# Experts' rows summed in open PSUM banks instead of scattered through HBM, with the overflow pass moved to the middle and two norms taken from one power step

## The chip, the core and the metric

The kernel runs on one NeuronCore of a Trainium2 chip. Its time is the device time of one execution in microseconds (us). The core has a matrix engine (TensorE, in the rows PE, with its weight loads as PEld), a vector engine (VectorE, DVE), a scalar engine (ScalarE, ACT), GpSimd (POOL), and a queue engine (SyncE, SP) that only starts transfers here. Each runs its own instruction list in order, and semaphores tie them together. Transfers between HBM and SBUF share 16 DMA engines. Matmuls write into PSUM, which has 8 banks of 128 x 512 f32.

## What is computed

A block of a language model on 256 tokens of 1024 channels: a first layer with two sequence mixers, then a mixture of experts, a norm, a second layer with a pooling mixer, and a wide convolutional FFN. Cut to what matters here:

```
x = x + gate1 * mix                       # end of the sequence mixers
h2 = modulate(rmsnorm(x, norm2_w), shift2, scale2)
# experts: top group of 4, then top 2 of its 8 experts for each token
hid = silu(xs @ w1[e]) * (xs @ w3[e])     # w1, w3: 32 x 1024 x 512, f32
ys = (hid @ w2[e]) * gate                 # w2: 32 x 512 x 1024, f32
ffn = segment_sum(ys, token)              # two rows for every token
x = rmsnorm(x + gate2 * ffn, final_norm_w)
h = rms_norm(x, norm_mix_g_2)             # a norm of a norm
x = x + pool_mixer(h)
x = x + conv_ffn(rms_norm(x, norm_ffn_g_2))   # 1024 -> 2 x 2816 -> 1024
```

The weights of the 32 experts are 6 MB each, 192 MB in all, and each is read once. Each token has 2 rows, so an expert has 16 rows on average.

## The kernel before

The program is one list per engine, written by hand; what stands first on an engine runs first. **The order of the stages** is: the mixers (to about 285 us of the span), the routing (to about 304), the experts (to about 805), the norms and the pooling mixer (to about 851), the FFN (to the end).

**Routing.** The normed rows are stored by ACT to HBM as `rows_scratch`, twice, one copy for each of a token's two choices (L1578). DVE and PE work out for every expert a block of 64 slots: `places(blk)` (PE L748, DVE L1202) turns rank and expert into `idx`, the token for each slot. Block 0 is needed before the first expert. Blocks 1 to 3 serve only an overflow, experts with more than 64 rows, and are made by an "aside" after the fourth expert (i == 3), together with `fcol`, the turned taps of the FFN.

**Experts.** For expert i POOL gathers 64 rows with an indirect DMA (L1832), four experts ahead. PE turns them (`turn_x`, L793), DVE scales and shifts them (L1258, L1261). PE does `up(i)` (L804 for w1, L807 for w3, side by side in the two halves of the array; every f32 matmul is two instructions), ACT the silu (L1607), DVE the product (L1269), PE `turn_h` (L817), DVE a copy (L1275), PE `down(i)` (L827, L828), DVE the product with gate2 (L1283), and POOL scatters the 128 half rows into `pair_scratch` in HBM (L1838). PE's order in one turn of the loop is up(i+1), turn_h(i), turn_x(i+2), down(i), [aside at i == 3]. PSUM banks are taken in turn, all eight.

**Weights.** SP loads w1, w3 and w2 in halves of 1 MB (L1990, L1992) into 7 slots of 2 MB, in the order w2(i), w1(i+2), w3(i+2). A load waits until PE has used the half that lies in its slot, and SP stands still in order behind it: first halves of w1 behind `down_half(i)`, of w3 behind `up_half(i+2)`.

**Behind the experts** each engine reads the overflow flag and jumps over the overflow pass (96 more blocks), which these inputs don't need. POOL waits for all scatters and sets `joined` (L1824). ACT then loads the pairs back (L1618, 4 x 512 KB). DVE adds them to X with their gates (L1308, L1313), multiplies by the final norm's weight (L1317), and ACT takes the sums of squares (L1416, L1625). The norm of a norm takes two power steps one after the other: POOL (L1697, L1699) takes a power, DVE refines it in four steps (`newton`, L949 to L955). ACT scales the rows for the mixer (L1629). PE, after idle matmuls (`turn_over`, L424), does the mixer's band products (L860, L861, L865) and the pooled products (L877). Then come the third norm, its transposes (L887), and the FFN. Its matmuls (L891 to L893) are fp32r on a high and a low part: ACT casts the high part (L1637), DVE subtracts for the low one (L1373; the first is POOL's, L1873). SP loads the mixer's constants (`late`, L2028, and `pool_w`, L2031) and the FFN's weights (L2052) only after the pairs are in.

## Time and profile before

| | us |
|---|---|
| three runs | 1046.86, 1050.27, 1054.45 (median 1050.27) |
| the profiled execution's own time | 1045.93 |
| its span | 1044.1 |
| mean granted TensorE clock | 0.967 |

| engine | busy, us | share of the span |
|---|---|---|
| PE | 910.6 | 87% |
| DVE | 365.8 | 35% |
| ACT | 199.0 | 19% |
| POOL | 176.1 | 17% |

In 40 slices of 26 us each (digits are tenths, DMA is the busy share of the 16 DMA engines):

```profile
PE   7997999999968979998788887887887489999998
DVE  1244412232342242222121121221221557888843
PEclk9998999999989979999999999999999689999999
DMA  9968326367596999999999999999994884555511
```

From slice 13 to 30 the DMA engines are full: these are the experts' weights. There PE is busy for some 80%, and a share of 80% says that it waits, not for whom. Slice 31 is the stretch after the last expert, where PE is nearly idle. From slice 33 on PE is full and DMA half used: the FFN. A gain in one of these stages is read from the wait that ends last in that stage.

### The profile page before, as it was taken

To read this page: it belongs to the slowest core of one execution; us is meant where nothing else is said; L and a number is where in the kernel's file an instruction comes from. 1 tells how busy PE (TensorE), PEld (TensorE's weight loads), DVE (VectorE), ACT (ScalarE), POOL (GpSimd) and SP (SyncE) were. 2 spreads that over 40 slices of the span, in tenths; PEclk is the share of its full clock that TensorE was granted. 3 is DMA by queue.
4 is the path that set the end of the run, shared out by engine and by line. 5 is a ranking of instruction groups with operands and counts; after the bars stand their busy time and mean duration, and the time that the engine had idled before them with its cause. 6 is when DMAs were issued, how large, how long until landed. Compare 5 with 4: busy or idle time off the path is not lost.

```text
span 1044.1 us, 11655 instructions
## 1 busy us (share of the span) xinstructions
PE 910.6 (87%) x4763; PEld 557.1 (53%) x4763; DVE 365.8 (35%) x631; ACT 199.0 (19%) x296; POOL 176.1 (17%) x188
## 2 busy tenths in 40 slices
PE   7997999999968979998788887887887489999998
PEld 5785656664533443443233232332332379999987
DVE  1244412232342242222121121221221557888843
ACT  1125211211120000000000000000000335555532
POOL 0000645021020120110111101101101222232300
PEclk9998999999989979999999999999999689999999
DMA  9968326367596999999999999999994884555511
GB/s 344 254 167 229 125 81 212 112 242 282 203 385 238 416 405 401 406 401 399 404 410 409 421 404 398 410 414 408 409 419 171 277 278 140 183 163 186 211 47 41
DMA packets 91349, 300.26 MB, mean 288 GB/s; under 512 B 13451, under 2 KB 37507, under 8 KB 66583
## 3 DMA queue, kind: packets, MB, share of 16 engines
q1 hardware_dynamic: 82295, 286.63, 73.4%
q10 hardware_dynamic: 3872, 8.58, 2.2%
q0 software_dynamic: 5120, 4.22, 1.4%
q8 instruction: 40, 0.66, 0.3%
q14 instruction: 22, 0.18, 0.0%
HBM read 300.43 MB, written 11.53 MB: 299 GB/s over the span
## 4 chain that ended last, share of the span: by engine, by line
PE 59%; DMA 33%; DVE 2%; ACT 2%; issue 2%; POOL 1%; ACTq 0%; SPq 0%; POOLq 0%; DVEq 0%
DMA ring<-in_w_dram 19%; DMA arena<-in_w_dram 11%; PE ps L804 7%; PE ps L440 7%; PE ps L891 6%; PE ps L892 6%; PE ps L893 6%; PE ps L807 4%; PE ps L429 4%; PE ps L514 4%; PE ps L827 3%; PE ps L691 3%; PE ps L424 2%; PE ps L450 2%; PE ps L466 1%
## 5 line engine op out<-in xcount | busy, mean ns | idle before, releaser
L807 PE MATMUL ps<-ring,proj 128*64 128x512 f32 x288 | 129.8, 596 | 26.0 <-DMA ring<-in_w_dram 26.0
L1269 DVE TENSOR_TENSOR proj<-RQ,ps 64x512 f32<-64x512 f32 x32 | 22.1, 690 | 298.8 <-ACT RQ L1607 268.0
L804 PE MATMUL ps<-ring,proj 128*64 128x512 f32 x272 | 124.3, 597 | 0.2 <-DMA ring<-in_w_dram 0.2
L807 PE MATMUL ps<-arena,proj 128*64 128x512 f32 x224 | 105.1, 617 | 20.1 <-DMA arena<-in_w_dram 20.1
L804 PE MATMUL ps<-arena,proj 128*64 128x512 f32 x240 | 113.6, 616 | 3.6 <-issue 3.6
L1607 ACT ACTIVATE RQ<-ps 64x512 f32<-64x512 f32 x32 | 18.9, 591 | 472.2 <-PE ps L807 472.2
L1838 POOL DMA_INDIRECT pair_scratch<-MX,idx x32 | 32.4, 1012 | 424.4 <-DVE MX L1283 424.4
L891 PE MATMUL ps<-h_h,w_h 128*128 128x256 f32 x352 | 101.0, 287 | 1.7 <-DVE h_l L1365 1.7
L892 PE MATMUL ps<-h_l,w_h 128*128 128x256 f32 x352 | 100.8, 286 | 0.0
L893 PE MATMUL ps<-h_h,w_l 128*128 128x256 f32 x352 | 100.8, 286 | 0.0
L1373 DVE TENSOR_TENSOR w_l<-ring,w_h 128x2048 fp32r<-128x2048 f32 x32 | 73.3, 2292 | 50.6 <-ACT w_h L1637 50.6
L807 PEld LDWEIGHTS ps<-ring,proj 128*64 128x64 f32 x288 | 37.4, 137 | 83.5 <-DMA ring<-in_w_dram 46.1
L827 PE MATMUL ps<-ring,proj 128*64 128x512 f32 x152 | 68.7, 595 | 13.9 <-issue 13.9
L1637 ACT CAST w_h<-ring 128x2048 fp32r<-128x2048 f32 x33 | 62.8, 1902 | 88.6 <-PE ps L893 86.7
L440 PE MATMUL ps<-ring,hT 128*128 128x512 f32 x160 | 70.0, 592 | 0.0
L891 PEld LDWEIGHTS ps<-h_h,w_h 128*128 128x128 f32 x352 | 68.9, 196 | 1.9 <-issue 1.9
L828 PE MATMUL ps<-ring,proj 128*64 128x512 f32 x152 | 69.3, 598 | 0.0
L892 PEld LDWEIGHTS ps<-h_l,w_h 128*128 128x128 f32 x352 | 68.9, 196 | 0.0
L893 PEld LDWEIGHTS ps<-h_h,w_l 128*128 128x128 f32 x352 | 68.8, 196 | 0.0
L807 PEld LDWEIGHTS ps<-arena,proj 128*64 128x64 f32 x224 | 30.0, 141 | 64.5 <-DMA arena<-in_w_dram 36.0
L827 PE MATMUL ps<-arena,proj 128*64 128x512 f32 x104 | 47.0, 595 | 9.2 <-issue 9.2
L1880 POOL TENSOR_TENSOR MX<-MX 128x256 f32<-128x256 f32 x22 | 36.5, 1661 | 108.4 <-ACT MX L1667 108.4
(294 smaller groups left out, 1433.6 us busy)
## 6 DMA issues: line engine op xcount, KB each, us to landing
ring<-in_w_dram SPq DMA_DIRECT2D x108, 1024.0 KB, 28.2
arena<-in_w_dram SPq DMA_DIRECT2D x84, 1024.0 KB, 27.9
ring<-in_w_ada_dram SPq DMA_DIRECT2D x12, 2048.0 KB, 10.9
ring<-in_ffn_w_in_dram SPq DMA_DIRECT2D x22, 1024.0 KB, 7.7
ring<-in_w_in_dram SPq DMA_DIRECT2D x6, 2048.0 KB, 19.8
ring<-in_ffn_w_out_dram SPq DMA_DIRECT2D x5, 2048.0 KB, 7.7
arena<-in_w_in_dram SPq DMA_DIRECT2D x2, 2048.0 KB, 25.5
ring<-in_w_out_dram SPq DMA_DIRECT2D x2, 2048.0 KB, 9.9
```

The costliest lines, as they stand in the source:

```text
L429: i = pe.matmul(ps[:, h * 128:(h + 1) * 128], lhs(h), rhs(h), start=True, stop=True)
L440: i = pe.matmul(ps[:, 0:512], hT[:, k, tok(n)], w[:, k, 0:512], start=(k == 0), stop=(k == 7))
L514: i = pe.matmul(ps[:, 0:256], w[:, k, m * 128:(m + 1) * 128], hT[:, k, :], start=(k == 0), stop=(k == 7))
L804: pe.matmul(ps[0:SLOTS, :], XTe[i % 2][:, k, :], u1[:, k, :], start=(k == 0), stop=(k == 7))
L807: t = pe.matmul(ps[64:64 + SLOTS, :], XTe[i % 2][:, k, :], u3[:, k, :], start=(k == 0), stop=(k == 7))
L827: pe.matmul(ps[0:SLOTS, :], HTe[i % 2][:, k, :], u2[:, k, 0:512], start=(k == 0), stop=(k == 3))
L828: t = pe.matmul(ps[64:64 + SLOTS, :], HTe[i % 2][:, k, :], u2[:, k, 512:1024], start=(k == 0), stop=(k == 3))
L891: pe.matmul(ps, ah, bh, start=first, stop=False)
L892: pe.matmul(ps, ah, bl, start=False, stop=False)
L893: return pe.matmul(ps, al, bh, start=False, stop=final)
L1373: ve.tensor_tensor(low, src, dst.bitcast(F32), ALU.subtract).then_inc(split_ready, 1)
L1637: ac.copy(dst, src).then_inc(w_high, 1)
```

## The change

It takes the detour through `pair_scratch` away. Each expert's result is multiplied by its gate and by gate2 on DVE (`YG`), split into a high part (ACT, two casts) and a low part (DVE, two subtractions), which lie one over the other in 128 partitions. DVE makes a 0/1 matrix `SPREAD` from `row_of`, and PE's `combine(i)`, 4 fp32r matmuls of 128 x 512, adds the rows to their tokens in 4 PSUM banks that stay open from expert 0 to expert 31. The other 4 banks serve everything else. The gates must therefore be known for each slot: `shares(blk)` makes `gate_of` in the manner of `places(blk)`. The overflow pass stands after expert 15, so the list of each engine has its jump there, and expert 16 starts like the first (weights of 16 and 17 behind w2(15)). `rows_scratch` is stored once. The two norms come from one power step on two columns. The mixer's constants and the FFN's first weights are loaded when w2(31) is in. The product of the pooling bias moves from POOL to DVE, the first low part from POOL to DVE; the third norm works in halves of the row, and the FFN's first step does all high products before the low ones.

```diff
+def weights_after(i):
+
+
+    if i == MIDDLE - 1:
+        return MIDDLE, MIDDLE + 1
+    return (i + 2,) if i + 2 < NE and i != MIDDLE - 2 else ()
...
+                for blk in range(1, NBLK):
+                    places(blk)
+                    shares(blk)
+
             places(0)
             gate_total(10, late_part[0])
             gate_total(11, late_part[1])
+            shares(0)
             turn_over(10)
-            tensor_experts(pe, main, lambda: tensor_aside(pe, take, places))
...
+            def combine(i):
+
+                if not acc:
+                    acc.extend(take("x2", n, j, keep=True) for n in range(2) for j in range(2))
+                pe.wait_ge(E.spread_ready, i + 1)
+                pe.wait_ge(E.low_rows, 2 * i + 2)
+                first, final = E is main and i == 0, E is main and i == NE - 1
+                for n in range(2):
+                    for j in range(2):
+                        t = pe.matmul(acc[2 * n + j][:, :], SPREAD[i % 2][:, tok(n)], YB[i % 2][:, j, :], start=first, stop=final)
+                        if final:
+                            t.then_inc(*mm.up("x2", n, j))
+                if not final:
...
+                if i + 1 < high:
                     up(i + 1)
                 turn_h(i)
-                if i + 2 < N:
+                if i + 2 < high:
                     turn_x(i + 2)
+                if i > low:
+                    combine(i - 1)
                 down(i)
                 if aside and i == 3:
                     aside()
+            combine(high - 1)
...
             pe.wait_ge(mix_rows, 1)
             for c in range(8):
                 ps, g, cc = take("mix", c), c // 2, slice(c * 128, (c + 1) * 128)
                 pss.append(ps)
-                pe.matmul(ps[:, 0:128], MX[:, 0, cc], band[:, g, 0:128], start=True, stop=True)
-                pe.matmul(ps[:, 128:256], MX[:, 0, cc], band[:, g, 128:256], start=True, stop=False)
+                pe.matmul(ps[:, 0:256], MX[:, 0, cc], band[:, g, 0:256], start=True, stop=False)
...
+            for a in range(2):
+                for k in range(8):
+                    pe.matmul(pss[a][:, 0:256], wh[:, k, a, :], HL[:, k, :], start=False, stop=False)
+            split(0)
+            for a in range(2):
+                for k in range(8):
...
+                ve.wait_ge(*vd.now())
+                for i in range(4):
+                    k, n = i // 2, i % 2
+                    ve.wait_ge(*mm.of("places", blk, i))
+                    ve.tensor_scalar(Q[i], cst("places"), slot[:, k, n:n + 1], gate[:, k, n:n + 1], ALU.is_equal,
+                                     ALU.mult).then_inc(shares_ready, 1)
+                ve.wait_ge(*mm.of("shares", blk, 3))
+                ve.tensor_copy(of_block(gate_of, blk), PS[banks.at["shares", blk][0]][:, 0:NE]).then_inc(*free("shares", blk))
...
+            shares(0)
...
+                    shares(blk)
+                ve.wait_ge(finals_in, 48)
+                ve.tensor_tensor(v_pb, v_pb, v_psc, ALU.mult).then_inc(*vd.up("bias_scaled"))
...
-                ve.tensor_tensor(YS[i % 4], ps[:, :], g2x[:, :], ALU.mult).then_inc(*free("down", i))
...
+                if i:
+                    ve.wait_ge(E.low_rows, 2 * i)
+                ve.scalar_tensor_tensor(YG, ps[:, :], gate_of[:, col:col + 1], g2x, ALU.mult, ALU.mult).then_inc(*free("down", i))
+                if i > 1:
+                    ve.wait_ge(*E.mm.of("combine", i - 2))
+                ve.tensor_scalar(SPREAD[i % 2], rows, row_of[:, col:col + 1], None, ALU.is_equal).then_inc(E.spread_ready, 1)
+                for j in range(2):
+                    own, other = slice(64 * j, 64 * j + 64), slice(64 - 64 * j, 128 - 64 * j)
+                    ve.wait_ge(E.high_rows, 2 * i + j + 1)
+                    ve.tensor_tensor(YB[i % 2][other, j, :], YG[own, :], YB[i % 2][own, j, :].bitcast(F32),
+                                     ALU.subtract).then_inc(E.low_rows, 1)
...
+                    xj = X[:, n, 512 * j:512 * j + 512]
+                    ve.tensor_tensor(xj, xj, full("x2", n, j)[:, :], ALU.add).then_inc(*free("x2", n, j))
...
+                ve.wait_ge(*drained("x2", n, 1))
                 ve.tensor_tensor(V[n], X[:, n, :], v_fin, ALU.mult).then_inc(*vd.up("weighted", n))
...
+                ve.wait_ge(first_sq, n + 1)
+                ve.tensor_scalar(m[:, 0:1], ss[:, n:n + 1], 1.0 / 1024, 1e-6, ALU.mult, ALU.add).then_inc(*vd.up())
+                ve.tensor_scalar(t, ss[:, n:n + 1], 1e-6 / 1024, 1e-12, ALU.mult, ALU.add).then_inc(*vd.up())
                 ve.wait_ge(*vd.now())
                 ve.wait_ge(second_sq, n + 1)
...
+                ve.scalar_tensor_tensor(m[:, 1:2], sv[:, n:n + 1], 1.0 / 1024, t, ALU.mult, ALU.add).then_inc(*vd.up("means", n))
+
+            def both_norms(n):
+                newton(both[:, n, :], [pair_m[n]] + [q[:, 0:2] for q in tms[n][1:]])
+                vd.at["norms", n] = vd.n
+
+            second_residual(0)
+            second_residual(1)
+            mean_squares(0)
+            both_norms(0)
+            mean_squares(1)
...
-                for k in range(2):
-                    r0 = 256 * k + 128 * n
-                    ac.dma_start(xs[r0:r0 + 128, :], MX[:, n, :]).then_inc(rows_stored, 16)
+                ac.dma_start(xs[tok(n), :], MX[:, n, :]).then_inc(rows_stored, 16)
...
+                for j in range(2):
+                    own = slice(64 * j, 64 * j + 64)
+                    ac.copy(YB[i % 2][own, j, :], YG[own, :]).then_inc(E.high_rows, 1)
...
-                    r0 = 512 * q + 256 * n
-                    ac.dma_start(YP[:, q, n, :], ys[r0:r0 + 256, :].rearrange("(p h) c -> p (h c)", h=2)).then_inc(pairs_in[n], 16)
...
-            ac.wait_ge(pairs_in[1], 32)
-            high(0)
             for c in range(1, 8, 2):
                 ac.activation(hT[:, c, :], full("mix", c)[:, 0:256], ACT.Copy, scale=fcol[:, 176 + c:177 + c]).then_inc(*free("mix", c))
+            high(0)
...
             with po.If(some > 0):
-                gpsimd_experts(po, more, None)
-                for i in range(4):
-                    po.wait_ge(more.scattered[i], 16 * (len(more.jobs) // 4))
...
-            def scatter(i):
-                col = E.jobs[i][0] * NBLK + E.jobs[i][1]
-                po.wait_ge(*E.drained("down", i))
-                po.indirect_dma_start(ys, bass.IndirectOffsetOnAxis(ap=idx[:, 1, col:col + 1], axis=0), YS[i % 4], None,
-                                      bounds_check=1023, oob_is_err=False).then_inc(E.scattered[i % 4], 16)
...
+
+            for n in range(2):
+                po.wait_ge(*vd.of("means", n))
+                root(tms[n][1][:, 0:2], pair_m[n])
...
+            for i in range(MIDDLE - 1):
+                load_rest(i)
+            load_halves(("w2", MIDDLE - 1))
             sp.wait_ge(overflow_known, 1)
             some = sp.value_load(flag_i[0:1, 0:1], min_val=0, max_val=1)
             with sp.If(some > 0):
-                sp.wait_ge(*mm.of("down", NE - 1))
...
-            sp.wait_ge(pairs_in[1], 32)
-            sp.wait_ge(pairs_in[0], 32)
-            s, _ = units.at["late",]
-            sp.wait_ge(*used(units.before["late",]))
+            for k in weights_after(MIDDLE - 1):
+                load_halves(("w1", k), ("w3", k))
+            for i in range(MIDDLE, NE):
+                load_rest(i)
+            sp.wait_ge(*filled(("w2", NE - 1)))
+            s, _ = units.at["mixer",]
+            sp.wait_ge(*used(units.before["mixer",]))
             sp.dma_start(slots[s][:, 0:1536], I["late"]).then_inc(slot_full[s], 16)
```

**DVE, the aside after the fourth expert.** Before, from the product of `down(3)` (L1283) on; L1202 are four operations of `places`.

```order
L1283 TENSOR_TENSOR MX<-ps,hT 128x512
L1234 COPY S<-ps 128x192
L1196 TENSOR_SCALAR part<-part 128x4
L1202 TENSOR_SCALAR S<-consts,part 128x128 x4
L1207 TENSOR_SCALAR idx<-ps 128x32
L1208 TENSOR_SCALAR idx<-ps,consts 128x32
L1196 TENSOR_SCALAR part<-part 128x4
L1202 TENSOR_SCALAR S<-consts,part 128x128 x4
L1207 TENSOR_SCALAR idx<-ps 128x32
L1208 TENSOR_SCALAR idx<-ps,consts 128x32
L1196 TENSOR_SCALAR part<-part 128x4
```

In the changed kernel, from the same product (now L1363) to the second block; L1262 is `places`, L1279 and L1282 are `shares`.

```order
L1363 SCALAR_TENSOR_TENSOR RQ<-ps,gate_of,hT 128x512
L1366 TENSOR_SCALAR RQ_r<-consts,row_of 128x256
L1370 TENSOR_TENSOR MX_r<-RQ,MX_r 64x512 x2
L1309 COPY S<-ps 128x192
L1256 TENSOR_SCALAR part<-part 128x4
L1262 TENSOR_SCALAR S<-consts,part 128x128 x4
L1267 TENSOR_SCALAR idx<-ps 128x32
L1267 TENSOR_SCALAR row_of<-ps 128x32
L1279 TENSOR_SCALAR S<-consts,part,S 128x128 x4
L1282 COPY gate_of<-ps 128x32
L1256 TENSOR_SCALAR part<-part 128x4
L1262 TENSOR_SCALAR S<-consts,part 128x128 x4
```

Three more operations stand ahead of the aside, and each block has five operations more and one hand-over to PE and back more. The third block ends as the second does, and the product of the pooling bias (128 x 1024) follows.

**PE, between expert 15 and 16.** Before, the end of `down(15)` and the start of `up(17)`:

```order
L827 MATMUL ps<-ring,proj 64x512
L828 MATMUL ps<-ring,proj 64x512
L827 MATMUL ps<-ring,proj 64x512
L828 MATMUL ps<-ring,proj 64x512
L804 MATMUL ps<-arena,proj 64x512
L807 MATMUL ps<-arena,proj 64x512
L804 MATMUL ps<-arena,proj 64x512
L807 MATMUL ps<-arena,proj 64x512
```

In the changed kernel, the end of `down(15)`, `combine(15)` (L874), the flag, the jump, and `turn_x(16)` (L824):

```order
L859 MATMUL ps<-ring,proj 64x512
L858 MATMUL ps<-ring,proj 64x512
L859 MATMUL ps<-ring,proj 64x512
L858 MATMUL ps<-ring,proj 64x512
L859 MATMUL ps<-ring,proj 64x512
L858 MATMUL ps<-ring,proj 64x512
L859 MATMUL ps<-ring,proj 64x512
L874 MATMUL ps<-MX_r,RQ_r 128x512 x4
L789 TENSOR_LOAD flag_i
L789 ISA x2
L790 COMPARE_AND_BRANCH
L824 MATMUL ps<-consts,proj 128x64 x8
```

The list is cut here: `combine(15)` waits for DVE's work on `down(15)`, and `up(16)` stands behind the jump and a new `turn_x`.

**DVE, behind the last expert.** Before, the last two experts' work (L1283 is the product of `down`), the end of the overflow pass (the branch), and the sums of the first tokens:

```order
L1275 COPY proj<-ps 128x256
L1283 TENSOR_TENSOR MX<-ps,hT 128x512
L1275 COPY proj<-ps 128x256
L1283 TENSOR_TENSOR MX<-ps,hT 128x512
L1241 UNCONDITIONAL_BRANCH
L1308 SCALAR_TENSOR_TENSOR X<-arena,S,X 128x1024
L1313 SCALAR_TENSOR_TENSOR X<-arena,S,X 128x1024
L1317 TENSOR_TENSOR arena<-X,S 128x1024
```

In the changed kernel, the last expert's work and the sums:

```order
L1355 COPY proj<-ps 128x256
L1363 SCALAR_TENSOR_TENSOR RQ<-ps,gate_of,hT 128x512
L1366 TENSOR_SCALAR RQ_r<-consts,row_of 128x256
L1370 TENSOR_TENSOR MX_r<-RQ,MX_r 64x512 x2
L1395 TENSOR_TENSOR X<-X,ps 128x512 x2
L1399 TENSOR_TENSOR arena<-X,S 128x1024
L1395 TENSOR_TENSOR X<-X,ps 128x512 x2
L1399 TENSOR_TENSOR arena<-X,S 128x1024
L1405 TENSOR_SCALAR S<-S 128x1
L1406 TENSOR_SCALAR S<-S 128x1
L1409 SCALAR_TENSOR_TENSOR S<-S 128x1
```

The pairs' loads are gone from between the last product and the first sum; what stands there now is SPREAD and two subtractions, with PE's `combine(31)` behind them.

## Rows read from the trace of the kernel before

**Rows 1.** Windows: span, PE, PEld, DVE, ACT, POOL busy (count), clock, DMA share, GB/s

```profile
390.00:400.00 10.00, 9.06 (x44) 3.24 (x42) 1.54 (x3) 0.59 (x1) 0.00 (x0) 0.84 0.96 380
...
600.00:700.00 100.00, 81.80 (x373) 31.33 (x374) 18.57 (x30) 3.55 (x6) 11.81 (x12) 1.00 1.02 406
```

**Rows 2.** Timeline of SP: start, duration, queue and line, transfer, count

```profile
362.45 5.48 SPq L1992 DMA_DIRECT2D ring<-in_w_dram  x2
...
374.93 0.33 SPq L1992 DMA_DIRECT2D ring<-in_w_dram  x1
...
394.31 0.33 SPq L1992 DMA_DIRECT2D arena<-in_w_dram  x1
```

**Rows 3.** DMA answer, 400 to 760 us: POOL's queue; its issues, median us to landing

```profile
q0 software_dynamic: 3689, 3.47, 3.2%
...
pair_scratch<-MX,idx POOLq DMA_INDIRECT x24, 6.7
...
proj<-rows_scratch,idx POOLq DMA_INDIRECT x23, 7.4
```

**Rows 4.** Timeline, the aside: start, us, engine, line, form, [idle before <- releaser]

```profile
377.72 3.95 DVE L1202 TENSOR_SCALAR S<-consts,part 128x128 f32<-128x128 f32 x4
...
379.24 2.35 POOL L1811 TENSOR_TENSOR vrow<-vrow,gates 128x1024 f32<-128x1024 f32 x1
...
382.87 1.12 DVE L1202 TENSOR_SCALAR S<-consts,part 128x128 f32<-128x128 f32 x4
...
385.75 1.12 DVE L1202 TENSOR_SCALAR S<-consts,part 128x128 f32<-128x128 f32 x4
...
388.06 1.12 PE L804 MATMUL ps<-arena,proj 128*64 128x512 f32 x1
```

**Rows 5.** Timeline of PE ahead of `down(3)`

```profile
372.96 0.61 PE L827 MATMUL ps<-ring,proj 128*64 128x512 f32 x1 [0.46 <-issue]
```

**Rows 6.** Timeline of PE in the FFN, two fp32r matmuls of 256 columns

```profile
861.01 0.28 PE L891 MATMUL ps<-h_h,w_h 128*128 128x256 f32 x1
...
861.13 0.28 PE L892 MATMUL ps<-h_l,w_h 128*128 128x256 f32 x1
```

**Rows 7.** Timeline of PE around the first expert

```profile
301.30 4.48 PE L424 MATMUL ps<-consts 128*128 128x256 f32 x20
...
314.71 1.08 PE L804 MATMUL ps<-arena,proj 128*64 128x512 f32 x1 [1.66 <-issue]
```

**Rows 8.** Timeline of PE from the last expert's weights to the FFN

```profile
791.25 0.64 PE L807 MATMUL ps<-arena,proj 128*64 128x512 f32 x1 [1.19 <-DMA arena<-in_w_dram]
...
821.01 5.49 PE L424 MATMUL ps<-consts 128*128 128x256 f32 x12 [15.64 <-ACT MX L1625]
...
828.05 0.46 PE L860 MATMUL ps<-ring,MX 128*128 128x128 f32 x2 [1.56 <-issue]
...
835.25 7.14 PE L877 MATMUL ps<-ring,hT 128*128 128x256 f32 x32 [1.60 <-ACT hT L1646]
...
851.49 0.55 PE L891 MATMUL ps<-h_h,w_h 128*128 128x256 f32 x1 [1.72 <-DVE h_l L1365]
```

**Rows 9.** Timeline of DVE behind the last expert

```profile
805.40 0.69 DVE L1283 TENSOR_TENSOR MX<-ps,hT 128x512 f32<-128x512 f32 x1 [3.79 <-PE ps L828]
...
818.55 1.23 DVE L1317 TENSOR_TENSOR arena<-X,S 128x1024 f32<-128x1024 f32 x1
...
826.74 0.16 DVE L949 TENSOR_TENSOR S<-S 128x1 f32<-128x1 f32 x1
```

**Rows 10.** Timeline of ACT behind the last weights

```profile
794.94 0.59 ACT L1607 ACTIVATE RQ<-ps 64x512 f32<-64x512 f32 x1 [14.64 <-PE ps L807]
...
829.78 1.15 ACT L1629 ACTIVATE MX<-arena,S 128x1024 f32<-128x1024 f32 x1 [1.82 <-DVE S L1332]
```

**Rows 11.** Timeline of POOL behind the last scatter

```profile
810.79 0.10 POOL L1824 MEMSET S<- 128x1 f32 x1 [2.95 <-DMA pair_scratch<-MX,idx]
...
826.16 0.55 POOL L1699 TENSOR_TENSOR S<-S,consts 128x1 f32<-128x1 f32 x1
```

371 lines of the change are left out of this document (187 added, 184 removed).

## The prediction

> **What bounds the kernel now.** I read the stages first, then in each stage the wait that ends last.
>
> The windows [rows 1] show the experts' stage: from 600 to 700 us the DMA engines are full (share 1.02, 406 GB/s) and PE works for 81.80 of 100 us. An expert's weights are 6.29 MB. POOL's queue takes 3.47 MB in 360 us [rows 3], 10 GB/s, so weights come at 396 GB/s and an expert takes 15.9 us. When the weights are there, PE needs 12.48 us for an expert: the distance of two issues of SP that stand behind `down_half(2)` and `down_half(3)` [rows 2].
>
> Only while PE leads does it stand on the path: SP then waits for a slot. This happens at the start, when all 7 slots are full, and once more behind the aside. SP issues at 374.93 and then stands until 394.31 behind `up_half(5)` [rows 2], and from 390 to 400 us the DMA share has its one dent, 0.96 and 380 GB/s [rows 1]. So 19.4 us of issued transfers just about covered a pause of 19.4 us. **Whatever makes the aside longer leaves the DMA engines idle one for one.** After it PE gains 15.9 - 12.48 = 3.4 us per expert on the DMA engines, until it waits for weights.
>
> From 791.25 (PE gets the last first-stage weights) to 851.49 (first FFN matmul) the path is one chain through all engines [rows 8 to 11]. Behind it the FFN is PE's own work.
>
> **The change part by part**, against the profiled execution (span 1044.1, time 1045.93; the median, 1050.27, is 0.4% higher).
>
> *Start: -2 us.* One store instead of two lets the gathers land earlier, but PE now runs `shares(0)`, which waits for the gates, ahead of its 20 idle instructions (301.30 to 305.78 [rows 7]). I put these some 4 us later, partly at half clock, so `turn_x(0)` starts about when it does now, behind the gathers. What changes is the pause before: now PE stands from 305.78 on, and `up(0)` starts at half clock (1.08 us for an instruction that takes 0.61 warm [rows 7, 5]). In the new order the idle work ends where the experts start. Four pairs of matmuls at 0.47 less each: 2 us. Bounds 0 and -4.
>
> *`combine`: +0.5 us per expert on PE, hidden behind the weights.* Two fp32r matmuls of 256 columns start 0.12 us apart [rows 6]; 512 columns are 0.24, four of them 1.0 us. They stand ahead of `down(i)`, where PE waits 0.46 for DVE [rows 5]. The period becomes 13.0, well under 15.9. DVE's and ACT's work for `combine(i-1)` (about 3 us) has `up(i+1)` before it: 16 pairs of 512 columns at twice 7.14/32 [rows 8], 7.1 us. It counts three times ahead of the aside: +1.5.
>
> *The aside: +6.9 us with the two above.* DVE's `down(3)` is now product, ACT's cast, two subtractions: 0.69 + 0.59 + 2 x 0.69 [rows 9, 10] and three hand-overs of 0.1, against 0.69: +2.3. Three blocks of `shares`: a block of `places` takes 385.75 - 382.87 = 2.88 [rows 4], `shares` has the same four operations and hand-over and one short operation less, 2.65 each: +7.9. Against that, the four operations of block 1 took 3.95 instead of 1.12, while POOL multiplied the bias for 2.35 [rows 4]; POOL has no such work any more: -2.8. Together: -2 + 1.5 + 2.3 + 7.9 - 2.8 = +6.9, so `up(5)` starts at 395.0 instead of 388.06 [rows 4], and SP goes on at 401.2. The DMA engines ran dry at 394 before and now run dry no later: all of it is exposed. Bounds: `shares` from 1.4 us a block (the wait for PE alone) to 3.95: +3 to +11.
>
> *No scatters: -5.4 us.* 24 of them went with 23 gathers in 360 us, in 3.2% of the DMA engines' time [rows 3]. Half of that on the 397 us from 394.31 to 791.25 is 6.4 us. By bytes, 24 x 32 rows of 2 KB, 1.57 MB at 396 GB/s in 360 us, it is 4.4. I take the middle. Bounds 0 and -8.
>
> *The jump between expert 15 and 16: 0.* `combine(14)` and `combine(15)` each wait about 3 us for DVE and ACT, the new `turn_x(16)` and `turn_x(17)` 1.7 us each (as at the start [rows 7]), and the flag and the jump come on top. A jump on an idle chip costs POOL at most the 2.95 us before its memset [rows 11]. That is 12 us of pause. The cover: with 13.0 us for PE against 15.7 for the DMA engines, PE's lead has shrunk by 27 us since the aside, and more than 20 us of slots are free to load. DMA never stops. Bounds 0 and +10.
> The Trainium skill, Runtime: NRT & Kernel Launch, section Instruction fetch mechanics, says that a taken branch outside the two pages at hand forces a DMA fetch of the target before execution goes on. No row shows such a fetch. By the rows the sum has 0 here, by the rule up to +12: it is rival 1.
>
> *From 791.25 to the first band product: -7.2 us.* PE's end shifts first: `combine(30)` stands between `turn_h(31)` and `down(31)` with DVE's 3 us ahead of it, +2.7, so `down(31)` ends at 808.1. Then 3.0 (DVE, ACT, DVE), 0.5 for the first two matmuls, 1.4 for two sums, 1.23 for the weights, 2.6 for the second tokens: 816.8. The means 0.6, the power 0.55 and hand-overs 0.4, four steps of 0.19: 819.1; ACT's scaling 1.15: 820.3 [rows 9 to 11]. PE's 12 idle instructions start behind ACT's squares at 815.4 and take 5.49 cold [rows 8]: 820.9. Before: 828.05. The constants are there: SP issues them when w2(31) is in, about 800, instead of after the pairs.
> *To the pooled products: -1.5 us.* 16 band products of 256 columns at 4.48/20 and 16 of 128 at half: 5.6 us, to 826.5. Before 7.2, because ACT's cast of the FFN's weights stood ahead of its `hT` copies.
> *To the first FFN matmul: +0.4 us.* The third norm now starts on DVE behind all sums, and both its powers come one after the other (+2); the first products need no low part (-1.5). 826.5 + 16.2 + 0.5 = 843.2, against 851.49 [rows 8]. Together -8.3; bounds -4 and -11.
>
> **Sum:** 6.9 - 5.4 + 0 - 8.3 = -6.8 us: span 1037.3, time 1039.1, a ratio of 0.9935. On the median 1050.27 that is **1043.4 us**.
>
> **Rivals.**
> 1. *The jump is dear.* Fetches for PE and DVE queue with the weights; a small transfer of POOL's lands in 7.4 us then [rows 3]. One on the path makes the pause 17 us, still under 20; two or three, 25 to 32, leave the DMA engines idle for 5 to 12. For it: before, the jump stood where everything waited anyway. Against: the lead. By this 1049 to 1055. The skill's rule above names the mechanism. Chance 0.10, a third of it slower by over 1%.
> 2. *PE becomes the bound (slower).* If `combine` ran at f32 speed, two instructions of 0.45 for each product (512 columns at twice 7.14/32 [rows 8]), it would take 3.6 us and the period would be 12.48 + 3.6 - 0.46 = 15.6, as long as the DMA engines'. Then the aside starts 7 us later than I say, PE's lead never shrinks, the jump's 12 us are exposed, and the last two combines cost 3 more: +15 to +18, 1063. It beats the gain from about 2.3 us per combine. For it: banks that stay open and a stationary side that is new each time. Against: 0.12 us in rows 6. Chance 0.06.
> 3. *The aside costs half.* If DVE and PE overlap the two kinds of block, or the DMA engines still had work at 394, +3 instead of +7, and with scatters at -7: -12 to -13, 1038. For it: a dent of only 0.04. Against: every Q waits for the matmul that reads it. Chance 0.24, most of it faster by over 1%.
> 4. *The change does less than it says at the end*: the clock stays at half through the shorter chain, or casts and subtractions take longer than their shapes say: -4 instead of -8.3, 1047. Chance 0.12, no change.
>
> The forecast itself has 0.48. Differences under 1%, 10 us, can't be told from none here. Faster by over 1% (under 1039.8): most of rival 3 and a part of the forecast: 0.28. Slower (over 1060.8): rival 2 and a third of rival 1, and a remainder: 0.11. Within: 0.61. The range takes in rival 3 with its bounds (-15) and the dear jump (+5): 1034 to 1055.
>
> **What would show it.** SP's issue behind the aside at about 401 instead of 394, and a DMA window below 0.5 before it; `up(5)` at 395. Scatters gone and 15.6 to 15.7 us per expert later. Two `combine` matmuls 0.24 apart. No SP wait of more than 2 us near expert 16. First band product 29.7 us behind the last wait for expert weights (now 36.8), first FFN matmul 52 us behind it (now 60.2). Wrong if PE stops waiting for weights after the jump (rivals 1, 2), if SP's pause behind the aside stays at 19 us (rival 3), or if the FFN's start is less than 5 us nearer (rival 4).

## The result, and the profile after

The changed kernel takes 1036.52 us (median of 4 runs, 1033.95 to 1037.30), the kernel before 1048.96 in the same comparison: a ratio of 0.987, with a 95% interval of 0.983 to 0.991. A second comparison gave 1037.12 us (6 runs) and 0.989 (0.988 to 0.991); the two medians are 12.4 and 11.9 us below the kernel before. The forecast was 1043.4 us: the direction and the range hold, the gain is about twice as large. The profiled execution has a span of 1032.1 us (before 1044.1).

The two windows of [rows 1], in the trace after. Behind the aside the DMA engines stand; from 600 to 700 us they are full as before, and PE works for 96 of 100 us.

```profile
390.00:400.00 10.00, 9.04 (x36) 5.32 (x38) 3.49 (x12) 0.00 (x0) 0.00 (x0) 0.63 0.16 66
600.00:700.00 100.00, 96.27 (x464) 40.56 (x459) 33.52 (x56) 12.79 (x21) 6.54 (x7) 1.00 1.02 408
```

SP's issues, which answer to [rows 2] (start, duration, line, transfer). SP now stands from 374.6 to 399.68, 25.1 us instead of 19.1.

```profile
361.20 5.48 SPq L2070 DMA_DIRECT2D ring<-in_w_dram  x2
...
374.29 0.33 SPq L2070 DMA_DIRECT2D ring<-in_w_dram  x1
399.68 0.33 SPq L2070 DMA_DIRECT2D arena<-in_w_dram  x1
```

POOL's queue from 400 to 760 us, against [rows 3]: the gathers alone take 1.7% (packets, MB, share; then the gathers, median us to landing).

```profile
q0 software_dynamic: 1760, 1.68, 1.7%
...
proj<-rows_scratch,idx POOLq DMA_INDIRECT x22, 7.2
```

The aside on DVE, against [rows 4]. From `places(2)` at 384.41 to `places(3)` at 389.74 a block takes 5.33 us: 2.62 up to the operations of `shares` (L1279), 2.71 from there to the next block. The stall of 3.95 us is gone: in `places(1)` they take 1.11.

```profile
379.42 1.11 DVE L1262 TENSOR_SCALAR S<-consts,part 128x128 f32<-128x128 f32 x4
...
384.41 1.11 DVE L1262 TENSOR_SCALAR S<-consts,part 128x128 f32<-128x128 f32 x4
...
387.03 1.11 DVE L1279 TENSOR_SCALAR S<-consts,part,S 128x128 f32<-128x128 f32 x4
...
389.74 1.12 DVE L1262 TENSOR_SCALAR S<-consts,part 128x128 f32<-128x128 f32 x4
```

PE around the first expert, against [rows 7]: `turn_x(0)` starts at the moment when the idle work (L439) ends, and `up(0)` runs at full clock.

```profile
305.32 6.18 PE L439 MATMUL ps<-consts 128*128 128x256 f32 x20
311.43 1.09 PE L824 MATMUL ps<-consts,proj 64*128 64x64 f32 x8
314.18 0.61 PE L835 MATMUL ps<-arena,proj 128*64 128x512 f32 x1 [1.66 <-issue]
```

PE in the middle: `combine(15)`, then `turn_x(16)` behind the jump and `up(16)`; under it a window over the pause (DMA share 1.02).

```profile
562.34 1.18 PE L874 MATMUL ps<-MX_r,RQ_r 128*128 128x512 f32 x4 [3.09 <-DVE MX_r L1370]
569.38 1.11 PE L824 MATMUL ps<-consts,proj 64*128 64x64 f32 x8 [5.86 <-issue]
572.08 1.09 PE L835 MATMUL ps<-ring,proj 128*64 128x512 f32 x1 [1.59 <-issue]
```

```profile
560.00:570.00 10.00, 1.80 (x10) 1.32 (x11) 1.69 (x4) 1.23 (x2) 0.00 (x0) 0.73 1.02 418
```

PE from the last expert's weights to the FFN, against [rows 8]: last wait for weights, `combine(30)`, `combine(31)`, idle work, first band product, pooled products, first FFN matmul.

```profile
788.97 0.64 PE L838 MATMUL ps<-arena,proj 128*64 128x512 f32 x1 [1.33 <-DMA arena<-in_w_dram]
...
801.31 1.18 PE L874 MATMUL ps<-MX_r,RQ_r 128*128 128x512 f32 x4 [2.46 <-DVE MX_r L1370]
...
809.16 1.17 PE L874 MATMUL ps<-MX_r,RQ_r 128*128 128x512 f32 x4 [3.09 <-DVE MX_r L1370]
813.55 4.64 PE L439 MATMUL ps<-consts 128*128 128x256 f32 x12 [3.21 <-ACT MX L1731]
818.09 3.69 PE L908 MATMUL ps<-ring,MX 128*128 128x256 f32 x16
...
823.40 7.07 PE L923 MATMUL ps<-ring,hT 128*128 128x256 f32 x32
...
840.19 3.75 PE L954 MATMUL ps<-h_h,w_h 128*128 128x256 f32 x16 [0.77 <-ACT h_h L1763]
```

**All kernels by stage.** Spans can't be compared to better than some us, and the three profiles that matter most lie apart from their medians: the kernel before (1045.93 us) and the first of the changed kernel (1033.95) are below, the second (1039.46) is above. SP's first issue of expert weights, t0, falls anywhere between 274.6 and 280.6 us, though nearly all that runs up to there is the same in all of them. So the stages are read from marks in each trace: t1 is SP's first issue behind `up_half(0)`, t3 PE's last wait for expert weights (both as in the rows above), "band" and "FFN" the first band product and first FFN matmul, counted from t3. All in us.

| kernel | t0 | t0 to t1 | t1 to t3 | band | FFN | FFN to end | span | median |
|---|---|---|---|---|---|---|---|---|
| before | 277.85 | 42.23 | 471.17 | 36.80 | 60.24 | 192.61 | 1044.1 | 1047.5 to 1049.0 |
| changed | 276.07 | 41.80 | 471.10 | 29.12 | 51.22 | 191.91 | 1032.1 | 1036.52 |
| changed, again | 277.69 | 41.79 | 471.73 | 32.31 | 54.22 | 192.17 | 1037.6 | 1037.12 |
| no_shares | 277.61 | 41.66 | 467.93 | 30.67 | 52.86 | 191.74 | 1031.8 | 1030.30 |
| late_aside | 275.95 | 43.45 | 472.25 | 32.50 | 54.36 | 192.29 | 1038.3 | 1037.14 |
| apart | 279.82 | 41.87 | 462.69 | 30.72 | 52.72 | 192.00 | 1029.1 | 1030.54 |
| no_jump | 274.63 | 43.47 | 471.95 | 30.51 | 52.69 | 191.66 | 1034.4 | 1036.26 |
| no_scatter | 280.14 | 44.10 | 462.53 | 38.50 | 62.25 | 191.48 | 1040.5 | 1039.78 |
| idle_short | 278.80 | 39.07 | 471.96 | 31.28 | 53.08 | 192.29 | 1035.2 | 1038.32 |
| idle_again | 278.56 | 38.57 | 472.41 | 29.13 | 51.32 | 191.84 | 1032.7 | 1036.92 |
| two_steps | 278.07 | 41.65 | 473.24 | 30.32 | 52.49 | 192.55 | 1038.0 | 1038.96 |
| down_first | 280.58 | 41.78 | 471.03 | 29.84 | 51.75 | 192.06 | 1037.2 | 1038.17 |
| turn_first | 277.83 | 41.80 | 472.11 | 26.11 | 48.29 | 191.67 | 1031.7 | 1033.96 |
| best | 277.77 | 38.56 | 463.05 | 27.14 | 46.94 | 189.98 | 1016.3 | 1019.63 |

### The profile page after: what moved, and what is told of

It reads as the page before. It is cut to its first block, busy times and chain, and to the rows that moved or that the text cites. A ratio compares the mean times of both kernels' runs of the same rounds, so it can differ in the third digit from the quotient of the medians.

```text
span 1032.1 us, 12126 instructions
## 1 busy us (share of the span) xinstructions
PE 942.9 (91%) x4907; PEld 583.0 (56%) x4907; DVE 421.3 (41%) x747; ACT 239.6 (23%) x364; POOL 131.9 (13%) x149
## 4 chain that ended last, share of the span: by engine, by line
PE 68%; DMA 20%; SPq 3%; DVE 3%; issue 2%; ACT 2%; POOL 0%; ACTq 0%; DVEq 0%
DMA ring<-in_w_dram 16%; PE ps L835 12%; PE ps L455 7%; PE ps L858 6%; PE ps L937 6%; PE ps L938 6%; PE ps L939 6%; PE ps L444 4%; PE ps L838 3%; PE ps L706 3%; DMA arena<-in_w_dram 3%; SPq L1990 3%; PE ps L874 2%; PE ps L465 2%; PE ps L439 1%
## 5 line engine op out<-in xcount | busy, mean ns | idle before, releaser
L838 PE MATMUL ps<-arena,proj 128*64 128x512 f32 x240 | 109.9, 608 | 7.9 <-DMA arena<-in_w_dram 7.9
L835 PE MATMUL ps<-arena,proj 128*64 128x512 f32 x240 | 109.0, 601 | 5.5 <-issue 5.5
L937 PE MATMUL ps<-h_h,w_h 128*128 128x256 f32 x336 | 95.1, 283 | 0.0
L938 PE MATMUL ps<-h_l,w_h 128*128 128x256 f32 x336 | 95.1, 283 | 0.0
L939 PE MATMUL ps<-h_h,w_l 128*128 128x256 f32 x336 | 95.1, 283 | 0.0
L1714 ACT CAST MX_r<-RQ 64x512 fp32r<-64x512 f32 x64 | 39.5, 618 | 202.4 <-DVE RQ L1363 201.6
L1941 POOL DMA_INDIRECT proj<-rows_scratch,idx x32 | 30.2, 944 | 399.6 <-PE ps L824 389.5
L937 PEld LDWEIGHTS ps<-h_h,w_h 128*128 128x128 f32 x336 | 64.5, 192 | 0.0
L938 PEld LDWEIGHTS ps<-h_l,w_h 128*128 128x128 f32 x336 | 64.5, 192 | 0.0
L939 PEld LDWEIGHTS ps<-h_h,w_l 128*128 128x128 f32 x336 | 64.5, 192 | 0.0
L1363 DVE SCALAR_TENSOR_TENSOR RQ<-ps,gate_of,hT 128x512 f32<-128x512 f32 x32 | 24.0, 751 | 98.1 <-PE ps L859 98.1
## 6 DMA issues: line engine op xcount, KB each, us to landing
ring<-in_w_ada_dram SPq DMA_DIRECT2D x12, 2048.0 KB, 10.9
```

Of the source, the lines that this page charges most:

```text
L835: pe.matmul(ps[0:SLOTS, :], XTe[i % 2][:, k, :], u1[:, k, :], start=(k == 0), stop=(k == 7))
L838: t = pe.matmul(ps[64:64 + SLOTS, :], XTe[i % 2][:, k, :], u3[:, k, :], start=(k == 0), stop=(k == 7))
L937: pe.matmul(ps, ah, bh, start=first, stop=False)
L938: pe.matmul(ps, ah, bl, start=False, stop=False)
L939: return pe.matmul(ps, al, bh, start=False, stop=final)
L1714: ac.copy(YB[i % 2][own, j, :], YG[own, :]).then_inc(E.high_rows, 1)
```

## The experiments

**The aside's length** (no_shares). In DVE's and PE's lists:

```
 for blk in range(1, NBLK):
     places(blk)
-    shares(blk)
```

> The changed kernel with the shares of blocks 1 to 3 left out (the gates of overflow rows are not computed; the data has no overflow). Theory A, as in the forecast: each block of shares costs about 2.5 us of the aside and each us of the aside is a us of idle DMA engines, so SP's pause falls from 25.4 us to about 18, and the total by 7.5 us, to 1029. Theory B (rival 3 of the forecast): DVE and PE overlap the two kinds of block, or the DMA engines have work left: the pause falls by less than 4 us, 1033 or more.

1030.30 us, ratio 0.983 (0.981 to 0.985). SP's pause is 17.8 us instead of 25.1, 7.3 less as expected: a block of shares costs 2.4 us. The window from 390 to 400 us has a DMA share of 0.82 instead of 0.16. But from t1 to t3 only 3.2 us are gained; the DMA engines now have a share of 0.92, 0.83 and 0.91 in the windows from 570 to 600 us, behind the jump. There SP stands for 22.4 us in this build, from 555.89 to 578.26, and for 17.5 in the changed kernel. PE's pause ahead of `turn_x(16)` is longer, 7.73 us against 5.86:

```profile
567.42 1.11 PE L823 MATMUL ps<-consts,proj 64*128 64x64 f32 x8 [7.73 <-issue]
```

Why the jump takes longer in this build is not shown. The rest of the gain in the medians is not seen in a stage; this profile is of the slowest of the four runs (1033.63). Theory A holds for the aside: its pause and the idle time of the DMA engines there fall as it says. What this run does not show is that the gain arrives in full at the end of the stage.

**The aside later** (late_aside).

```
-                if aside and i == 3:
+                if aside and i == 10:
```

> The changed kernel with the aside (fcol, and places and shares of blocks 1 to 3) behind down(10) instead of down(3). Theory A, the one of the forecast: at expert 3 PE leads, the transfers issued cover only part of the aside, and the DMA engines stand for about 9 us (window 390 to 400 us of the changed kernel: share 0.16). By expert 10 the slots freed and not yet loaded hold some 30 us of transfers (17.4 us at 374 us, and 15.5 - 13.1 = 2.4 us more for each expert), so a pause of 25 us leaves them running: no window of 10 us between 340 and 780 us with a DMA share below 0.95, last wait for expert weights 8 to 9 us earlier, total -8 us, about 1028 us. Perhaps 1 to 2 us come back at the jump behind expert 15, where the lead is then only some 19 us of transfers against SP's pause of 20. Theory B: the stage from 400 us on is bound by something that doesn't care when the DMA engines stood (PE was 96 per cent busy from 600 to 700 us): then less than 3 us come back, 1034 us or more.

1037.14 us, ratio 0.989 (0.985 to 0.992): no gain. The windows show that neither theory is right (390 to 400 us, 480 to 500 over the aside, and behind the jump, columns as in [rows 1]):

```profile
390.00:400.00 10.00, 10.00 (x54) 4.04 (x51) 3.13 (x6) 1.83 (x3) 0.00 (x0) 1.00 1.02 394
480.00:490.00 10.00, 4.57 (x26) 3.80 (x23) 6.75 (x22) 1.24 (x2) 0.00 (x0) 0.80 1.01 397
490.00:500.00 10.00, 7.71 (x34) 6.71 (x35) 4.93 (x20) 0.00 (x0) 0.00 (x0) 0.50 1.01 420
...
570.00:580.00 10.00, 5.49 (x20) 2.45 (x22) 1.42 (x2) 0.00 (x0) 0.93 (x1) 0.50 0.66 266
580.00:590.00 10.00, 8.07 (x36) 3.25 (x34) 2.07 (x3) 0.59 (x1) 0.93 (x1) 0.84 0.65 218
590.00:600.00 10.00, 9.07 (x46) 3.62 (x44) 2.02 (x4) 0.59 (x1) 0.93 (x1) 0.91 0.77 293
```

At expert 10 the aside is covered in full, but the jump, five experts later, is not: 30 us at shares of 0.66, 0.65 and 0.77 are 9 us of standing engines, as much as the changed kernel loses from 390 to 410 us (0.16 and 0.94). I had put that return at 1 to 2 us. The next run tells whether the jump itself or its distance from the aside is to blame.

**Aside and jump apart** (apart): the edit above, and

```
-MIDDLE = NE // 2
+MIDDLE = 22
```

> The changed kernel with the aside behind down(10) and the jump behind expert 21 instead of 15. The version with the aside at 10 and the jump at 15 gained nothing: the DMA engines kept on through the aside, but stood from about 575 to 586 us, behind the jump (0.34 and 0.37 in two windows of 5 us). Theory A: both pauses draw on one store of transfers, which grows by 2.4 us per expert; five experts between them aren't enough, eleven are. No window of 10 us between 340 and 780 us below 0.95, last wait for expert weights 8 to 9 us earlier counted from SP's first issue behind up_half(0) (318 us): 462 instead of 471 us, total 1028. Theory B: the jump itself stops the DMA engines, wherever it is (its dent in that version was then no debt of the aside): the dent appears behind expert 21 again, and the total stays at 1034 or more.

1030.54 us, ratio 0.983 (0.980 to 0.986), and 462.69 us from t1 to t3, 8.4 less. The jump stands at about 650 us here, with PE busy for 2.17 of 10 us and the DMA engines full:

```profile
640.00:650.00 10.00, 7.72 (x20) 2.69 (x20) 2.01 (x4) 0.58 (x1) 0.00 (x0) 0.66 1.01 419
650.00:660.00 10.00, 2.17 (x12) 1.63 (x12) 1.37 (x2) 0.65 (x2) 0.00 (x0) 0.69 1.02 418
660.00:670.00 10.00, 8.41 (x27) 2.84 (x28) 1.42 (x2) 0.00 (x0) 0.93 (x1) 0.62 1.01 387
```

Only behind it is there a small dent, 0.94 and 0.95 from 670 to 690 us. SP's pause at the jump is as long as before, 19.4 us against 19.2 in late_aside, but the transfers issued just ahead of it take 26.6 us to land (median of three) and there 15.2 and 17.8. So both pauses draw on one store of issued transfers: theory A, though the total fell by 6, not 8. The store doesn't grow without end: in late_aside PE has caught up and waits for weights from 422 us on, and the transfers issued from 470 to 484 us land in 28 to 29 us.

**No jump** (no_jump): the overflow pass with its flag is left out, and the experts are one loop.

```
-            tensor_experts(pe, main, acc, 0, MIDDLE, aside)
-            pe.wait_ge(overflow_known, 1)
-            ...
-            tensor_experts(pe, main, acc, MIDDLE, NE, None)
+            tensor_experts(pe, main, acc, 0, NE, aside)
```

> The changed kernel without the overflow pass, its flag and its jumps (left out; the data takes none of it), and the experts as one loop of 32, so that there is no pause behind expert 15. Theory A (the forecast): the pause of about 12 us on PE is covered by transfers, the DMA engines never stop for it, and leaving it out changes nothing: last wait for expert weights 389 to 390 us behind SP's first issue after the aside, as in the changed kernel (389.3), total within 2 us of 1036.5. Theory B (rival 1 of the forecast): fetches of instructions or the shorter lead cost DMA time that the windows of 5 us hide: 3 us or more are gained, 1033 or less.

1036.26 us, ratio 0.989 (0.986 to 0.992), t1 to t3 471.95: nothing gained. PE's pause of 5.86 us is gone with it. Where the change has put it, the jump costs nothing.

**No scatters in the kernel before** (no_scatter): the main part of the edit. The waits for the scatters are left out as well, and the pairs are read from the stored rows.

```
             def scatter(i):
                 po.wait_ge(*E.drained("down", i))
+                if E is main:
+                    return
```

> The kernel before with all 32 scatters left out and the pairs read from the stored rows (so the experts' part of the output is left out); POOL still waits for each down(i) and does the rest. Theory A: the scatters alone made the stage from SP's issue behind the aside to the last wait for expert weights 7.6 us longer (396.9 against 389.3 us with the change), so it falls to 389 to 390 here too, and the total by 7 to 8 us plus some 2 for the wait for the last scatter, to about 1039. Theory B: it is worth the 5.4 us of the forecast (a middle between bytes and packets' time) and the other 2 us come from something else in the change: 391.5, total 1042. Theory C: the writes cost nothing beside the loads: 396 to 397.

1039.78 us, ratio 0.991 (0.987 to 0.994), 7.7 us less than before in the medians and 8.6 from t1 to t3. SP's queue (packets, MB, share of the DMA engines) from 405 to 780 us, first in the kernel before, then without scatters:

```profile
q1 hardware_dynamic: 20481, 149.14, 98.2%
```

```profile
q1 hardware_dynamic: 20789, 151.39, 99.6%
```

1.5% more weights in the same time: on the 397 us behind the aside that is 6.0 us for 26 scatters, 0.23 each. Four more lie ahead of the aside, two behind t3. So scatters account for some 7 of the 8.6 us; where the rest comes from no row shows. Theory A for the total; from SP's issue behind the aside to t3 it is 387.3 us (before 396.9), 2 us below what theory A gave. The wait for the last scatter isn't seen to go: the band product comes 1.7 us later behind t3 (38.50 against 36.80), and why is not shown.

**Idle work ahead of the experts** (idle_short, and idle_again beside after_again).

```
-            turn_over(10)
+            turn_over(3)
             acc = []
```

> The changed kernel with 3 instead of 10 idle matmuls (6 instead of 20 records) ahead of the experts. In the changed kernel turn_x(0) starts at 311.43 us, at the moment when the idle work ends, while its rows have been gathered some 4 us before; in the kernel before it was the gathers that came last. Theory A: the idle work is now on the path; turn_x(0) starts 4.3 us earlier (14 records of 0.31), the first pairs of up(0) run at half clock again (4 pairs at 0.47 more), and the total falls by 2 us (0 to 4). Theory B: the second kind of wait (weights or rows) ends last anyway, or the aside swallows it: no change.

> The version with 3 idle matmuls instead of 10 once more, beside the changed kernel on the same chip. Its profile had 39.1 us from the first issue of expert weights to SP's first issue behind up_half(0), against 41.7 for the others, and nothing lost up to the end; its median, 1038.3, showed no gain. Theory A: 2.7 us are gained and the first comparison had drawn a late first issue (278.8): now 2 to 3 us below the changed kernel of this call, 39 us again. Theory B: the idle work is paid back elsewhere: the same median as the changed kernel, within 1 us.

From t0 to t1 39.07 and 38.57 us instead of 41.8, and `turn_x(0)` starts 2.8 us behind the start of the idle work instead of 6.1. In the medians nothing is seen: 1038.32, ratio 0.991 (0.988 to 0.994), and 1036.92, 0.990 (0.988 to 0.992), beside 0.989 for the changed kernel in the second comparison. From t1 to t3 half a us to one comes back. The rows are those of idle_again: the start of the experts, and then the jump, where PE stands a second time inside `turn_x(16)`, for 5.21 us (5.33 in idle_short), so that SP's pause there is 20 us instead of 17.5 and the DMA share from 580 to 600 us is 0.98 and 0.96. So the jump takes 5 us longer here, though only the idle work ahead of the experts was changed; why is not shown. Why the medians show none of the 2 us that are left stays open.

```profile
306.17 2.91 PE L439 MATMUL ps<-consts 128*128 128x256 f32 x6
309.01 1.09 PE L824 MATMUL ps<-consts,proj 64*128 64x64 f32 x8
...
573.11 0.92 PE L824 MATMUL ps<-consts,proj 64*128 64x64 f32 x7 [5.21 <-issue]
```

**The changed kernel once more** (after_again).

> The changed kernel, unchanged, once more. By its first profile the experts' stage cost 471.1 us from SP's first issue behind up_half(0) to the last wait for expert weights, and 51.2 from there to the first FFN matmul, with down(31) at full clock. Theory A: what comes before the experts (274.6 to 280.6 us until the first issue of expert weights, in eight builds that are the same up to there) and the clock of down(31) differ from execution to execution and not from build to build: the stage between is 471 to 472 again, the first issue anywhere from 275 to 281, down(31) starts its four products at half clock about as often as not; median 1035 to 1038. Theory B: the first profile is typical of this build: first issue at 276, down(31) at full clock.

Theory A. The rows are the two last combines of this execution: 10.7 us apart instead of 7.85, with the same 2.46 and 3.1 us of waiting. Behind them a window over `down(31)` here (TensorE's clock 0.50, its level of 1.2 GHz), and last one in the first profile (1.00).

```profile
803.56 2.05 PE L874 MATMUL ps<-MX_r,RQ_r 128*128 128x512 f32 x4 [2.46 <-DVE MX_r L1370]
814.22 1.16 PE L874 MATMUL ps<-MX_r,RQ_r 128*128 128x512 f32 x4 [3.10 <-DVE MX_r L1370]
```

```profile
803.00:808.00 5.00, 4.44 (x10) 1.94 (x12) 0.75 (x2) 0.00 (x0) 0.00 (x0) 0.50 1.02 364
```

```profile
800.00:804.00 4.00, 2.69 (x12) 1.30 (x14) 1.47 (x3) 0.37 (x1) 0.00 (x0) 1.00 0.88 309
```

**Two power steps** (two_steps): for each half of the tokens

```
-                po.wait_ge(*vd.of("means", n))
-                root(tms[n][1][:, 0:2], pair_m[n])
+                for q, name in enumerate(("mean_one", "mean_two")):
+                    po.wait_ge(*vd.of(name, n))
+                    root(tms[n][1][:, q:q + 1], pair_m[n][:, q:q + 1])
```

> The changed kernel with the two norms of the mixer from two power steps of POOL, one behind the other for each half of the tokens, as the kernel before had them. In the changed kernel one power step for both takes 0.74 us and DVE stands 0.86 before it; with two, each half has one more mean, hand-over and power step (0.86) and four more steps of 0.19. Theory A: 1.6 us later for the first tokens and 1.6 more for the second, since DVE does one half after the other: the first band product waits for the first tokens, the second group for the second, and the first FFN matmul comes 2 to 3 us later, total +2 to +3, about 1039. Theory B: squares and idle matmuls hide it (PE's idle work ends at 818.19, where the first product starts): +0.5 or less.

1038.96 us, ratio 0.991 (0.988 to 0.994). Between `combine(31)` and the first band product 10.1 us instead of 8.9, and to the first FFN matmul 32.3 instead of 31.0: the single step is worth 1.3 us, half of theory A. Part of each step may lie beside the squares and the second tokens; that is not shown. The 1.5 to 2 us more from t1 to t3 lie ahead of the place that was changed.

**`down(31)` ahead of `combine(30)`** (down_first).

```
-                if i > low:
+                if i > low and i < high - 1:
                     combine(i - 1)
                 down(i)
+                if i > low and i == high - 1:
+                    combine(i - 1)
```

> The changed kernel with combine(i-1) behind down(i) instead of ahead of it for the last expert of each half (15 and 31). Theory A: ahead of down(31) PE stands 2.46 us for DVE's lower rows of expert 30 and then runs combine(30) for 1.18; with the order changed down(31) starts 3.6 us earlier and combine(30) fills part of DVE's and ACT's 3.1 us behind it. From the last wait for expert weights to the first band product 25.5 us instead of 29.1, total -3.6, about 1033 us; nothing at expert 15, where the pause is covered. Theory B: DVE and ACT, which finish expert 30 first, or the constants of the mixer come last: less than 1 us.

1038.17 us, ratio 0.990 (0.988 to 0.992): nothing gained. Theory A forgot DVE's queue: the copy for `turn_h(31)` (L1357) stands behind the work for expert 30, and `down(31)` waits for it, then at half clock:

```profile
804.18 1.40 DVE L1372 TENSOR_TENSOR MX_r<-RQ,MX_r 64x512 fp32r<-64x512 f32 x2 [0.48 <-ACT MX_r L1716]
805.50 0.41 DVE L1357 COPY proj<-ps 128x256 f32<-128x256 f32 x1
```

```profile
806.02 1.09 PE L858 MATMUL ps<-ring,proj 128*64 128x512 f32 x1 [2.75 <-issue]
```

**The copy first as well** (turn_first): in DVE's loop

```
-                turn_h(i)
+                if i == first or i < end - 1:
+                    turn_h(i)
                 if i + 2 < end:
                     turn_x(i + 2)
+                if i == end - 2:
+                    turn_h(i + 1)
                 down(i)
```

> As the version with combine(30) behind down(31), and DVE copies turn_h(31) ahead of its work for down(30) (the same for 15 and 14). In that version down(31) still stood for 2.75 us, until DVE had done the four operations for expert 30 that stood ahead of the copy in its queue. Theory A: DVE's queue was the only thing left; the copy now comes 0.1 us behind turn_h(31), down(31) starts some 3 us earlier, without a pause in which TensorE's clock falls, combine(30) fits behind it. From the last wait for expert weights to combine(31) 17.5 us (20.2 in the changed kernel where down(31) ran at full clock, 21.8 to 23.1 where it ran partly at half), total 1032 to 1034. Theory B: the chain for combine(31) waits for the work of expert 30 anyway: 20 us, 1036 to 1038.

1033.96 us, ratio 0.987 (0.984 to 0.991); from t3 to `combine(31)` 17.2 us (20.2 and 23.0 in the changed kernel). Theory A. The stage shows the gain; in the medians it is 2.6 to 3.2 us, and the four runs spread from 1031.54 to 1038.02. DVE's copy and `down(31)`, now behind a wait of 0.56 us and at full clock:

```profile
801.67 0.42 DVE L1357 COPY proj<-ps 128x256 f32<-128x256 f32 x1 [4.42 <-PE ps L848]
```

```profile
802.19 0.61 PE L858 MATMUL ps<-ring,proj 128*64 128x512 f32 x1 [0.56 <-issue]
```

**Together** (best): the edits of apart, idle_short and turn_first, and DVE's order for the third norm

```
-            third_mean(0)
             ffn_norm(0)
             third_mean(1)
+            scaled(0)
             ffn_norm(1)
+            scaled(1)
```

with `third_mean(0)` moved behind the sum for tokens 1, columns 0 to 511, and `scaled` the last two operations of `ffn_norm`.

> The changed kernel with everything that the runs point to: aside behind down(10), jump behind expert 21, 3 idle matmuls ahead of the experts, the last expert's down ahead of combine(30) with DVE's copy first, and for the third norm the mean of the first tokens behind their second sum's successor, so that POOL's power and the first tokens' norm overlap the second tokens' sums. Expected on top of the version with aside and jump apart (1030.5): start 2.7, tail 3 (more where the clock falls), third norm 1.5: 1023 to 1024 us, 2.3 per cent below the kernel before. If the gains of the start are taken back behind it (the aside no longer exposed, but PE and DMA otherwise bound), 1026.

**1019.63 us, ratio 0.973 (0.971 to 0.976)**, 10.9 below apart and 3.4 to 4.4 below what was expected. From t0 to t1 3.3 us less than there, to the first FFN matmul 5.8, and 2.0 behind it: the two turns of the third norm (L935) now stand 2.09 us apart instead of 3.11, and the first FFN products run at full clock, 2.15 us for sixteen where the changed kernel needs 3.75. The 2.0 behind the first FFN matmul were not in the expectation. The third norm's order was not run by itself. One us is left ahead of the band products: the idle work ends at 806.74, ACT's scaling at 805.68.

```profile
822.14 1.32 PE L935 MATMUL ps<-consts,MX 128*128 128x128 f32 x8 [1.08 <-DVE MX L1460]
824.23 1.32 PE L935 MATMUL ps<-consts,MX 128*128 128x128 f32 x8 [0.77 <-DVE MX L1460]
826.32 2.15 PE L956 MATMUL ps<-h_h,w_h 128*128 128x256 f32 x16 [0.77 <-ACT h_h L1774]
```

## Why the prediction was right in kind and short in size

The sum was -6.8 us and the profiled spans differ by -12.0. By stages: -1.8 ahead of t0, which is within the spread of t0 and not put down to the change; -0.4 from t0 to t1 (forecast -2); -0.1 from t1 to t3 (forecast +3.5); -9.0 to the first FFN matmul (-8.3); -0.7 behind it (0). With the second profile of the changed kernel the same stages, without t0, add up to -6.3 and not -10.2: that so many terms agree with the first is partly luck.

- **No scatters: the term that was mis-sized.** -5.4 was a middle between bytes (4.4) and half of the DMA engines' time for POOL's queue (6.4), taken for the stretch behind the aside alone. The run without scatters shows 6.0 there, so the second was the better measure and the middle spoiled it, and 8.6 from t1 to t3. The four scatters ahead of the aside, where the engines were full as well, are 1 us of the difference; 1.6 us are not placed.
- **The aside**: right in kind and 1.3 us too high. From t1 to SP's issue behind it are 81.81 us (before 74.23): +7.6, where the forecast's parts, without the start's -2, were +8.9. It begins 1.6 us later, and SP's pause is 6.0 longer. Moving it to where it is covered gives back 8.4. That SP goes on at 399.68 (forecast 401.2) and `up(5)` starts at 394.66 (395.0), with t0 1.8 us earlier than before, is partly luck: the aside came out shorter, and the start gave 0.4 us of its 2. Rival 3 (half price) is out as a mechanism, though its total, 1038, was the nearest: it had the scatters nearly right and the aside wrong. So the two great terms cancel, +8.4 and -8.6, where I had +8.9 and -5.4.
- **The start**: the mechanism held (`up(0)` at full clock) but not the gain. The idle work took 6.18 us and not 4.48, and became what `turn_x(0)` waits for; I had left it behind the gathers. With less of it t1 comes 2.7 to 3.2 us sooner.
- **`combine`**: right. SP's period is 13.09 (361.20 less 348.11; forecast 13.0), four matmuls take 1.18 us (forecast 1.0). Rival 2 is out.
- **The jump**: 0, right. PE's pauses, 2.46 ahead of `combine(14)`, then 3.09, 5.86 and 1.59, and 1.93 ahead of `up(17)`, make 14.9 us (forecast 12, for the same), and the DMA engines stay at 1.01 or more in every 10 us from 540 to 590. The 5.86 between `combine(15)` and `turn_x(16)` agree in kind with the Trainium skill (Runtime: NRT & Kernel Launch, Instruction fetch mechanics), by which a taken branch to code not at hand has to fetch it first. Transfers of that kind are on record: from 555 to 575 us the DMA engines carry the packets below, of kind instruction, and in the same window of no_jump there are none (in the whole execution q14 has 22 packets, and 15 without the jump). For which engine they are, no row says. Rival 1 is out at this place: its mechanism is there, its price is not. The covering was not wide: late_aside lost 9 us here, and the jump's pause was 2 us longer in no_shares and 5 in idle_short. The sign that I named was a wrong one: SP does stand near expert 16, for 17.5 us; what matters is whether the engines do.

```profile
q8 instruction: 2, 0.03, 0.7%
q14 instruction: 4, 0.03, 0.4%
```

- **The end**: band product 29.1 us behind t3 (29.7), first FFN matmul 51.2 (52). The second profile of the same kernel has 32.3 and 54.2, so the agreement is partly luck: the forecast had `down(31)` at full clock without saying so. The idle work (forecast 820.9) ended at 818.19, and ACT's scaling, behind POOL, at 817.99 (forecast 820.3), so the two were level and not 0.6 us apart; with the chain lengthened, in two_steps, PE stands for 1.40 us behind its idle work. Rival 4 (a gain of 4 here, by a clock at half) is not the first execution, but the second, with 6.0, lies between it and the forecast.

What stays open: the medians differ by 11.9 to 12.4 us, the stages t0 to the end by 10.2 with the first profile of the changed kernel and by 6.3 with the second. The kernel before was profiled once, in an execution faster than its median, and its own stages move too (its edited version has 44.1 against 42.2 from t0 to t1, and 62.3 against 60.2 to the FFN).

## What to carry to other kernels

Where a matmul engine leads a full stream of loads, each of its pauses is paid from one store of issued transfers that refills by the difference of the two periods, here 2.4 us per expert, up to some 28 us: count all pauses against it, and set them far apart, before pricing any one. A small indirect transfer beside a full stream costs its share of the engines wherever they are full, and a run without it measures that better than bytes do: 6.0 us behind the aside, against 4.4 by bytes and 6.4 by half of its queue's time. When one engine's order is changed, look at what stands ahead of the answer in the other engine's list.

## What had not been expected

- A pause of 2.46 us ahead of `combine(30)` left TensorE's clock at its upper level through `down(31)` in some executions and not in others: the distance of the last two combines is 7.84 or 7.85 us in three profiles with this tail and 9.25 to 10.79 in six. One and a half to three us of the total depend on that. With the pause cut to 0.56 us, in turn_first and best, `down(31)` ran at full clock in both.
- The start of the experts' loads, t0, moved by 6 us between builds that are the same up to there, and by 1.6 us between two executions of one kernel. Differences of spans below that say nothing; the distance from t1 to t3 repeated within 0.7 us in both kernels that were profiled twice.
- The jump's pause on PE isn't the same in every build: 5.83 and 5.86 us in the two profiles of the changed kernel, 7.73 in no_shares, and in idle_short 5.92 with a second one of 5.33. The edits of these two builds lie elsewhere in PE's list, so a change of code ahead of a jump can cost time at the jump.
